# Retention in chunks of 128 tokens with a fading state in place of the whole lower triangle, and the head norm's square queued one step ahead of its sum

## What is computed

```python
def retention_chunkwise(q, k, v, gamma):        # RET_CHUNK = 128, s = 512: four chunks
    ...
    def step(state, inp):
        q_i, k_i, v_i = inp
        inner = einsum('bhqd,bhkd->bhqk', q_i, k_i) * decay_mask      # gamma^(i-j), i >= j
        o = (einsum('bhqk,bhkv->bhqv', inner, v_i)
             + einsum('bhqd,bhdv->bhqv', q_i * xi, state))            # xi = gamma^(i+1)
        state = chunk_decay * state + einsum('bhkd,bhkv->bhdv', k_i * zeta, v_i)   # zeta = gamma^(127-i)
        return state, o

q_r = rotary(rq); k_r = rotary(rk) * 128 ** -0.5
ret = head_groupnorm(retention_chunkwise(q_r, k_r, rv, gamma), ret_gn_g)
ret_out = silu(rg) * ret            # then w_out with the attention's half, layernorm, feed-forward
```

## Time and profile before

| | us |
|---|---|
| median of three runs | 2085.1 (2084.9 to 2085.11) |
| the profiled execution | 2085.24 |
| its span from first to last instruction | 2083.3 |
| mean granted clock of TensorE | 0.998 |

### The profile page before, as it was taken

The page is one execution under the profiler, slowest core; times in us unless marked ns, Lnnn a source line. Parts: engine busy times, 40 slices in busy tenths (PEclk is TensorE's granted clock), DMA queues, the critical chain, the costliest instruction groups (busy, mean ns, idle before and its releaser), DMA issues. The chain is left out here.

```text
span 2083.3 us, 24654 instructions
## 1 busy us (share of the span) xinstructions
PE 2051.0 (98%) x9744; PEld 1691.8 (81%) x9744; DVE 1098.9 (53%) x1794; ACT 923.0 (44%) x1502; POOL 150.8 (7%) x207
## 2 busy tenths in 40 slices
PE   9999999999999999999999999999999999999997
PEld 6888788888888888788688888888888788888886
DVE  6655566565343444477586333337677586333336
ACT  5664334334232322366357243343566347233243
POOL 0000000000000000354000000000353000000000
PEclk9999999999999999999999999999999999999999
DMA  7332222333323322632332333322632332332321
GB/s 241 98 105 62 81 66 96 123 100 122 104 98 101 101 81 62 182 113 85 117 102 84 99 101 101 101 85 58 179 102 79 117 101 85 108 99 93 101 81 41
DMA packets 201518, 211.37 MB, mean 101 GB/s; under 512 B 7803, under 2 KB 181115, under 8 KB 201404
## 3 DMA queue, kind: packets, MB, share of 16 engines
q1 hardware_dynamic: 194544, 194.13, 29.9%
q0 software_dynamic: 6352, 15.24, 2.8%
q10 hardware_dynamic: 508, 0.43, 0.1%
HBM read 194.55 MB, written 8.95 MB: 98 GB/s over the span
## 5 line engine op out<-in xcount | busy, mean ns | idle before, releaser
L303 PE MATMUL ps<-Phi,wh 128*128 128x512 f32 (+1 forms) x1200 | 475.9, 397 | 9.3 <-DVE Plo L1291 5.0
L306 PE MATMUL ps<-Phi,wl 128*128 128x512 f32 (+1 forms) x1200 | 455.2, 379 | 0.6 <-DVE wl L272 0.6
L305 PE MATMUL ps<-Plo,wh 128*128 128x512 f32 (+1 forms) x1200 | 454.5, 379 | 0.0
L272 DVE TENSOR_TENSOR wl<-stage,wh 128x1024 fp32r<-128x1024 f32 x249 | 303.6, 1224 | 71.0 <-ACT wh L269 55.7
L269 ACT ACTIVATE wh<-stage 128x1024 fp32r<-128x1024 f32 (+2 forms) x252 | 260.2, 1041 | 172.1 <-PE ps L306 157.8
L303 PEld LDWEIGHTS ps<-Phi,wh 128*128 128x128 f32 x1200 | 226.2, 189 | 58.2 <-issue 19.2
L306 PEld LDWEIGHTS ps<-Phi,wl 128*128 128x128 f32 x1200 | 225.6, 188 | 44.5 <-DVE wl L272 1.0
L305 PEld LDWEIGHTS ps<-Plo,wh 128*128 128x128 f32 x1200 | 226.3, 189 | 40.6 <-issue 4.1
L303 PE MATMUL ps<-Qhi,wh 128*128 128x512 f32 (+1 forms) x680 | 256.5, 377 | 0.8 <-DVE Qlo L459 0.8
L306 PE MATMUL ps<-Qhi,wl 128*128 128x512 f32 (+1 forms) x680 | 254.4, 374 | 0.0
L305 PE MATMUL ps<-Qlo,wh 128*128 128x512 f32 (+1 forms) x680 | 254.4, 374 | 0.0
(11 more groups left out here) (303 smaller groups left out, 2935.4 us busy)
## 6 DMA issues: line engine op xcount, KB each, us to landing
stage<-in_w_ff SPq DMA_DIRECT2D x64, 1024.0 KB, 5.3
stage<-in_w_in SPq DMA_DIRECT2D x39, 1024.0 KB, 5.2
stage<-in_w_up SPq DMA_DIRECT2D x16, 1024.0 KB, 5.3
stage<-in_w_down SPq DMA_DIRECT2D x16, 1024.0 KB, 5.1
stage<-in_w_in SPq DMA_DIRECT2D x30, 512.0 KB, 4.8
stage<-in_w_out SPq DMA_DIRECT2D x12, 1024.0 KB, 5.1
stage<-in_w_bg SPq DMA_DIRECT2D x4, 1024.0 KB, 5.2
vrev<-H SPq DMA_DIRECT2D x2, 2048.0 KB, 13.0
```

What stands on the lines that cost most here:

```text
L272: t_lo = V.op(lambda e: e.tensor_tensor(lo, src, hi.bitcast(F32), ALU.subtract), st_landed[n, part], t_hi, w_free[u], sem=s_wlo)
L303: PE.op(lambda e: e.matmul(o, hi[:, k, c], x.hi[:, kx, tok], start=first, stop=False), t_hi, t_x or x.t[kx], list(waits), signal=False)
L305: PE.op(lambda e: e.matmul(o, hi[:, k, c], x.lo[:, kx, tok], start=False, stop=False), signal=False)
L306: return PE.op(lambda e: e.matmul(o, lo[:, k, c], x.hi[:, kx, tok], start=False, stop=last), t_lo, sem=s_wpe, signal=last)
```

## The change

For each head the queries are multiplied by gamma^(i+1) of their place in the chunk (`decayed`, DVE, in place; a new instruction), for head 0 at the start of `retention()`, for the others in the second step of the head before. Scores are made only within the four chunks (four products of 128 columns into one bank) and masked by one DVE instruction with gamma^-(j+1). The keys of chunks 0 to 2 are transposed by TensorE, and ACT copies them with gamma^(127-j) into `kT`. Three products with the values give each chunk's contribution; ACT copies the first into `Sr`, and DVE adds up the other two (state times gamma^128 plus contribution). The output gathers four inner products and three with the state in one bank. Buffers of alternate heads are two (`IT`, `kT`, `Sr`). The steps per head stay four (head 0: seven), and the last norm takes as many steps as before. `normed` yields after the square. The decay tables shrink to 256 columns per head (two heads in `accq`, two in `dec`), and a table of four columns (`kdec`) is loaded once.

```diff
+        def table(h, what):
+            tile, o = (accq, dec)[h // 2], 256 * (h % 2) + 128 * what
+            return bass.AP(tensor=tile[:, :].tensor, offset=o, ap=[[S, 128], [0, 4], [1, 128]])
...
+            if L == 0:
+                t_kd = SP.op(lambda e: e.dma_start(kdec, consts[:, C_KD:C_KD + 4]), sem=s_c[12], inc=16)
...
                 t = A.op(lambda e: e.activation(wk[:, :], yr[:, h, :], ACT.Square), t_o, t_fox, t_y[h - 1] if h else None)
+                yield
                 b = next_bank()
                 t = PE.op(lambda e: e.matmul(banks[b][:, :], ones[:, :], wk[:, :], start=True, stop=True), t, settled(b))
...
             def retention():
                 attention_over()
...
+                def decayed(h):
+                    q = rdst(h).rearrange("p (n c) -> p n c", n=4)
+                    t_q[h] = V.op(lambda e: e.tensor_tensor(q, q, table(h, 1), ALU.mult), t_r[h], t_dec[h])
+
+                decayed(0)
                 for h in range(4):
...
                     while t_r[4 + h] is None:
                         yield
-                    for pair in ((0, 1), (2, 3)):
...
-                            ts.append(PE.op(lambda e, h=h, j=j, b=b, c=c, w=w: e.matmul(
-                                banks[b][:, c:c + w], rdst(4 + h)[:, 128 * j:128 * j + 128], rdst(h)[:, 128 * j:S],
-                                start=True, stop=True), t_r[h], t_r[4 + h], free[b] if c == 0 else None))
...
-                            t = V.op(lambda e, h=h, j=j, b=b, c=c, w=w: e.tensor_tensor(
-                                IT[:, j, 0:w], banks[b][:, c:c + w], decay(h)[:, 0:w], ALU.mult), ts, t_dec[h], it_free)
...
+                    for n in range(3):
+                        t = PE.op(lambda e, h=h, n=n: e.transpose(banks[5][:, chunk[n]], rdst(4 + h)[:, chunk[n]], ident),
+                                  t_r[4 + h], free[5])
+                    t_kt = A.op(lambda e, h=h, kt=kt: e.activation(
+                        kt[:, :, :], banks[5][:, 0:384].rearrange("p (n c) -> p n c", n=3), ACT.Copy, scale=kdec[:, h:h + 1]),
+                        t, t_kd, gone)
+                    free[5] = t_kt
+                    for n in range(4):
+                        t = PE.op(lambda e, h=h, n=n: e.matmul(banks[4][:, chunk[n]], rdst(4 + h)[:, chunk[n]],
+                                                               rdst(h)[:, chunk[n]], start=True, stop=True), t_q[h], free[4])
+                    t_it = V.op(lambda e, h=h, it=it: e.tensor_tensor(
+                        it[:, :, :], banks[4][:, :].rearrange("p (n c) -> p n c", n=4), table(h, 0), ALU.mult), t, gone)
+                    free[4] = t_it
                     next(norm, None)
                     yield
                     for _ in range(0 if h else 3):
                         yield
                     while None in t_rv:
                         yield
-                    for j in range(4):
-                        w = S - 128 * j
...
+                    for n in range(3):
+                        t = PE.op(lambda e, h=h, n=n, kt=kt: e.matmul(
+                            banks[7][:, chunk[n]], kt[:, n, :], rv[:, n, 128 * h:128 * h + 128],
+                            start=True, stop=True), t_kt, t_rv, free[7])
+                    t_s = [A.op(lambda e, st=st: e.activation(st[:, 0, :], banks[7][:, 0:128], ACT.Copy), t, gone)]
+                    for n in (1, 2):
+                        t_s.append(V.op(lambda e, n=n, st=st, gamma=gamma: e.scalar_tensor_tensor(
+                            out=st[:, n, :], in0=st[:, n - 1, :], scalar=gamma, in1=banks[7][:, chunk[n]],
+                            op0=ALU.mult, op1=ALU.add), t, t_s[n - 1], gone))
+                    free[7] = t_s
+                    if h < 3:
+                        while t_r[h + 1] is None:
+                            yield
+                        decayed(h + 1)
+                    next(norm, None)
+                    yield
+                    for n in range(4):
+                        t = PE.op(lambda e, h=h, n=n, it=it: e.matmul(
+                            banks[6][:, chunk[n]], rv[:, n, 128 * h:128 * h + 128], it[:, n, :],
+                            start=(n == 0), stop=False, skip_group_check=True), t_it, t_rv, free[6])
+                    next(norm, None)
+                    yield
+                    for n in (1, 2, 3):
+                        t = PE.op(lambda e, h=h, n=n, st=st: e.matmul(
+                            banks[6][:, chunk[n]], st[:, n - 1, :], rdst(h)[:, chunk[n]],
+                            start=False, stop=(n == 3), skip_group_check=True), t_s[n - 1])
+                    read[h % 2] = t
                     t_o = A.op(lambda e, h=h: e.activation(yr[:, h, :], banks[6][:, :], ACT.Copy), t, t_fox)
                     free[6] = t_o
                     norm = normed(h, t_o)
                     yield
                 for _ in norm:
-                    yield
                     yield
```

More of the change, by code:

```diff
@@ L17 @@
 NEG = -1.0e30
-C_ID, C_BLK, C_GM, C_CM, C_COS, C_SIN, C_DEC, C_OH, C_END = 0, 128, 256, 384, 512, 1024, 1536, 3584, 4224
+C_ID, C_BLK, C_GM, C_CM, C_COS, C_SIN, C_DEC, C_KD, C_OH, C_END = 0, 128, 256, 384, 512, 1024, 1536, 2560, 2576, 3216
 V_G1, V_G2, V_MQ, V_MK, V_GB, V_GO, V_LN1G, V_LN1B, V_LN2G, V_LN2B, V_RG, V_BF, V_T5, V_END = (
@@ L37, in constants @@
     c[:, C_SIN:C_SIN + S] = np.sin(ang) * np.where(p < 64, 1.0, -1.0)[:, None]
-    d = (np.arange(S)[None, :] - p[:, None]).astype(np.float64)
     for h in range(4):
         lg = np.log(1.0 - 2.0 ** (-5.0 - h))
-        c[:, C_DEC + S * h:C_DEC + S * h + S] = np.where(d >= 0, np.exp(lg * np.maximum(d, 0)), 0.0)
+        c[:, C_DEC + 256 * h:C_DEC + 256 * h + 128] = np.where(p[None, :] >= p[:, None], np.exp(-lg * (p + 1.0))[:, None], 0.0)
+        c[:, C_DEC + 256 * h + 128:C_DEC + 256 * h + 256] = np.exp(lg * (p + 1.0))[None, :]
+        c[:, C_KD + h] = np.exp(lg * (127.0 - p))
     dist = 511 - np.arange(639)
@@ L1443, in build @@
         cs = at(f"x_cs", g0 + 94, [8, S])
-        dec = at(f"x_dec", g0 + 28, [128, 3, S])
-        IT = at(f"x_IT", g0 + 36, [128, 4, S])
+        dec = at(f"x_dec", g0 + 28, [128, S])
+        IT = [at(f"x_IT{i}", g0 + 30 + 2 * i, [128, 4, 128]) for i in range(2)]
+        kT = [at(f"x_kT{i}", g0 + 34 + 1.5 * i, [128, 3, 128]) for i in range(2)]
+        Sr = [at(f"x_Sr{i}", g0 + 37 + 1.5 * i, [128, 3, 128]) for i in range(2)]
+        kdec = rcol[:, 11:15]
         rg = at(f"x_rg", g0 + 44, [128, 4, S])
@@ L1452, in build @@
         parked = bass.AP(tensor=vrev.tensor, offset=vrev.offset, ap=[[S, 128], [128 * S, 8], [1, S]])
-        def decay(h):
-            return dec[:, h - 1, :] if h else accq[:, :]
+        def table(h, what):
+            tile, o = (accq, dec)[h // 2], 256 * (h % 2) + 128 * what
+            return bass.AP(tensor=tile[:, :].tensor, offset=o, ap=[[S, 128], [0, 4], [1, 128]])
         for L in range(2):
@@ L1599, in build @@
             gemm_tok(P, ev_rv)
-            t_fox, t_dec = [], [t_dec0]
+            t_fox, t_dec = [], [t_dec0, t_dec0]
             def attention_over():
                 t_fox.extend([Q.t[3], PT_free, pS_free, free[4:8], bias_read, yf_free])
-                t_dec.extend(3 * [SP.op(lambda e: e.dma_start(
-                    dec[:, :, :], consts[:, C_DEC + S:C_DEC + 4 * S].rearrange("p (a t) -> p a t", a=3)),
-                    t_fox, sem=s_l[2], inc=16)])
+                t_dec.extend(2 * [SP.op(lambda e: e.dma_start(dec[:, :], consts[:, C_DEC + S:C_DEC + 2 * S]),
+                                        t_fox, sem=s_l[2], inc=16)])
                 t_h[:] = [SP.op(lambda e: e.dma_start(H[:, :, :], parked), t_fox, r_free, sem=s_l[4], inc=16)] * 8
@@ L1624, in retention @@
                 attention_over()
-                it_free, norm = t_fox, iter(())
+                norm, t_q, read = iter(()), [None] * 4, [t_fox, t_fox]
+                chunk = [slice(128 * i, 128 * i + 128) for i in range(4)]
+                def decayed(h):
+                    q = rdst(h).rearrange("p (n c) -> p n c", n=4)
+                    t_q[h] = V.op(lambda e: e.tensor_tensor(q, q, table(h, 1), ALU.mult), t_r[h], t_dec[h])
+                decayed(0)
                 for h in range(4):
-                    t_it = []
+                    it, kt, st, gone = IT[h % 2], kT[h % 2], Sr[h % 2], read[h % 2]
+                    gamma = float((1.0 - 2.0 ** (-5.0 - h)) ** 128)
@@ L1628, in retention @@
                     while t_r[4 + h] is None:
                         yield
-                    for pair in ((0, 1), (2, 3)):
[L1631 to L1634, removed]
-                            ts.append(PE.op(lambda e, h=h, j=j, b=b, c=c, w=w: e.matmul(
-                                banks[b][:, c:c + w], rdst(4 + h)[:, 128 * j:128 * j + 128], rdst(h)[:, 128 * j:S],
-                                start=True, stop=True), t_r[h], t_r[4 + h], free[b] if c == 0 else None))
-                        for j in pair:
```

(10 more changed lines are left out.)

## The result

The changed kernel takes 2090.5 us (median of 11 runs, 2088.3 to 2091.2) against 2085.0 (11 runs beside it): +5.5 us, a ratio of 1.0025 with a 95% interval of 1.0017 to 1.0032. Forecast were 2088.9, +3.7. It is slower, by a little more than the 0.2% that had been called the limit of what can be told; a time within that limit had been given the higher chance (0.50), slower 0.41. The profiled execution took 2090.12 us, 4.9 more than that of before.

A forecast was written before the change was run, and what follows sets the result against it. The prediction took TensorE to bound the kernel at the retention heads. Its terms, -7.1 (work), -3.1 (waits gone), +10.9 (new wait) and +3.0 (clock), sum to +3.7: 2088.9 us, range 2083.0 to 2093.0.

The forecast's parts named there:

- TensorE's work: Retention heads: chunked products and transposes take 3.41 us a head instead of 4.30, saving 7.1 us over eight heads.
- Rival 3: Products of 128 columns: weight loads can't be hidden, 0.19 us apart instead of 0.11, 18 us more, 2107; chance 0.03.
- The prediction's loss of 11 us: Retention's short products: by the Trainium skill's figures, eight heads would lose some 11 us instead of gaining 7.
- Waits that go: Retention: TensorE's waits at the norm's sum and L1654 vanish with the square a step ahead of its sum, -3.1 us.
- DVE and ACT: Retention heads: DVE stays at 1.94 us a head; ACT gains 6.0 us of copies, put at nothing, being covered.
- Rival 4: Retention heads: the states wait for ACT's late copy, 2 to 5 us in all, 2091 to 2094; chance 0.08.
- The wait that comes: Head 0, both layers: scores wait for the query scaling behind DVE's backlog, 5.4 and 5.5 us, +10.9 us.
- Rival 2: Head 0's first step: DVE's queue is empty and the scaling ready, so no wait, 2075.0; chance 0.09.
- The clock: Behind the rests before head 0's scores: half speed for up to 3.7 us, 1.5 lost per layer, +3.0 us.
- Rival 1: Behind both rests: 3.7 us or more at half speed, 1.87 to 3.7 lost per layer, 2089.6 to 2093.3; chance 0.28.
- the forecast's case: Head 0, both layers: both waits come, with a total clock loss of 1.5 to 3.4 us, 2087.4 to 2089.3; chance 0.42.

The follow-up runs named there:

- e4_sq_only: The kernel before with only the norm's square put one step ahead of its sum; 2081.74 us, ratio 0.9985.
- e1_early: The changed kernel with head 0's queries scaled on DVE right after their rotary product; 2075.35 us, ratio 0.9955.
- e3: The changed kernel with head 0's queries scaled right after their rotary product and the norm's square and sum in one step again; 2080.97 us.
- e5: The changed kernel with six idle TensorE products between transposes and head 0's scores, only the first waiting; 2085.46 us, ratio 1.0002.
- e6: The kernel before with one idle DVE product in the retention's first step, for which head 0's scores wait; 2101.27 us.
- e8: The changed kernel with two idle TensorE products between the transposes and head 0's scores; 2088.5 us.
- e2_fill: The changed kernel with six idle TensorE products before head 0's scores, each waiting for the one before to end; 2088.1 us.
- e7: The changed kernel with head 0's scores and masking moved behind its three empty steps; 2078.08 us, ratio 0.9966.

## Why the prediction was right, and by how much it was off

*TensorE's work.* The forecast was -7.1 us, at 0.11 us for each instruction of 128 columns. In the changed kernel six take 0.83 (L1665) and eight 1.05 (L1681): less one duration of 0.27, 0.11 apart. From e4_sq_only to e1_early, which differ by the chunks and both have the square moved, the stretches shrink by 7.0. Rival 3 (0.19 each) is out, and with it the estimate from the Trainium skill's figures for short matmuls (TensorE: Matmul & The Clock Gate, Back-to-back issue gap), which had the chunks lose. The prediction's loss of 11 us comes out only when these figures of the Trainium skill are scaled to the 0.23 us measured at 512 columns; as they stand, with a straight line between them, they give an estimate of 6.5 us lost. Either has the wrong sign here.

*Waits that go.* -3.1 forecast, -3.0 in e4_sq_only. Not foreseen: without the early square the chunks would have made all eight norms wait (e3). The change contains both, so the sum was not hurt.

*DVE and ACT.* The copy of the keys takes 0.58 us and not 0.49, that of the state 0.28 and not 0.26. TensorE never waits for either: the waits view of the changed kernel has no row of L1665 or L1687. Rival 4 did not occur. The waits of the earlier trace rows are gone, and none is left inside the phase but that for the scaling.

*The wait that comes.* +10.9 forecast: scores at 1002.88. They start at 1002.64, 0.24 earlier, as all before them is 0.12 earlier. The two waits cost 10.4 us by the waits view, 10.7 from the end of the transposes' own columns (0.33 us behind their start) to the scores, and e1 shows them gone by moving one instruction. Rival 2 had the right price for a kernel without the backlog, 2075.0; e1 took 2075.35.

*The clock.* This is the term that was mis-sized. +3.0 was taken, 1.5 per layer, between nothing and 1.87. The low clock lasts 4.1 us of work in layer 0 and 3.9 in layer 1, more than the 3.7 of the kernel's start that gave the upper bound: 4.0 us lost by the clock, 3.7 by e5. The bound was taken from a rise at the kernel's start. Here the low stretch of 6.8 us began inside the rest, 2.7 and 2.9 us before its end, and how much of it would be left for the work stood in no row. The rule in the Trainium skill (TensorE: Matmul & The Clock Gate, HAM oscillation) that bursts with waits between them start slow each time is borne out in both layers.

*The sum.* -7.0 - 3.0 + 10.7 + 4.0 = +4.7, against +4.6 in the stretches. The profiled executions differ by 4.9, the medians by 5.5; what lies outside the stretches is, as far as the traces show it, mostly the wait for `f0kl`. Its cause stays open, and no term of the forecast had it. Of the 1.8 us between the +3.7 forecast and the +5.5 measured, 1.0 is the clock and 0.9 lies outside the stretches; the other terms nearly cancel.

Rival 1 (the clock pays in full, 2089.6 to 2093.3) is what happened by its own condition, a total loss of 3.4 us or more; the forecast's case had the same mechanism at a lower price. The time lies well inside the stated range because that range took in rival 1, not because the price was right. Rival 1 had 0.28, and slower 0.41, where more was due: after a fall with 2.6 us of rest at the kernel's end and with a rest of 5.4 ahead, nothing in the rows spoke for a loss below the bound.

## What to carry to other kernels

When a change puts a new instruction of another engine ahead of the bound engine's work, look at where that engine's queue stands at this moment, not at its share of busy time: DVE was busy for half of the span, and at this place it was 5 us behind. A lag that costs nothing as long as its reader comes later becomes a wait in full when something is put in front of it; the cure is to issue the new work where its input is made. A rest of TensorE of several us costs its clock too, here nearly two fifths on top of the wait.

## What the runs showed of the hardware

Rests of TensorE of 5.2 and 5.5 us in a stream of matmuls brought the granted clock from 1.00 to 0.50 for 6.8 us, in both layers of the changed kernel (5.15 and 5.21) and of e6 (5.48 and 5.54). Rests of 3.4 and 3.5 us did so for 3.4 us in e8.

Shorter rests do not sort by length. After 1.50 us (e2_fill) and 1.57 us (e6) at the wait for `f0kl` the clock was low for 3.4 us, and both times it fell only when TensorE was at work again, 0.2 and 1.1 us after the first product. After 2.03 us (the changed kernel) and 2.29 us (e8) at the same place, and after 1.73 us in e7, it stayed at 1.00. What else decides is not shown.

Filling the long rest with products that nobody reads kept the clock at 1.00 there and made the changed kernel 5.1 us faster (3.7 in the stretches). An fp32 instruction of 128 columns costs 0.11 us, a quarter of the 0.43 of one of 512, so 0.22 per product, in rows of six and eight: no floor shows at 128 columns.
